# A decoder trunk's opening: x read from a transposed copy, first weights in halves on two queues, norm sums by columns

## What is computed

```
x = x + 1/2 * SwiGLU_1(RMSNorm(x))
h = RMSNorm(x)
x = x + mixers(h) @ W_out
x = x + 1/2 * SwiGLU_2(RMSNorm(x))

rmsnorm(x, gain) = x * rsqrt(mean(x * x, axis=-1) + 1e-6) * gain
swiglu(x, w_gate, w_up, w_down) = (silu(x @ w_gate) * (x @ w_up)) @ w_down
```

## Time and profile before

| | us |
|---|---|
| three timed runs | 1137.74, 1138.39, 1138.44 |
| median | 1138.39 |
| the profiled execution | 1138.71 |
| its span on the core | 1136.9 |

### The profile page before, as it was taken

The page is one execution under the profiler, slowest core; times in us unless marked ns, Lnnn a source line. Parts: engine busy times, 40 slices in busy tenths (PEclk is TensorE's granted clock), DMA queues, the critical chain, the costliest instruction groups (busy, mean ns, idle before and its releaser), DMA issues.

```text
span 1136.9 us, 16092 instructions
## 1 busy us (share of the span) xinstructions
PE 1133.1 (100%) x5975; PEld 966.9 (85%) x5975; DVE 770.4 (68%) x1055; ACT 630.6 (55%) x941; POOL 70.3 (6%) x79
## 2 busy tenths in 40 slices
PE   9999999999999999999999999999999999999999
PEld 7888888888888888888888888888887888888887
DVE  5766666868768676655766856678676695766655
ACT  6644445666674564544564544466766745544542
POOL 3020000202000000000020200002110000000000
PEclk9999999999999999999999999999999999999999
DMA  9956654545544666656566555636445445656521
GB/s 324 319 175 198 187 192 140 185 136 198 148 148 152 219 223 187 193 177 219 172 169 228 185 185 186 200 98 220 148 163 172 182 154 183 222 185 202 193 86 37
DMA packets 138828, 207.34 MB, mean 182 GB/s; under 512 B 6898, under 2 KB 99876, under 8 KB 138756
## 3 DMA queue, kind: packets, MB, share of 16 engines
q1 hardware_dynamic: 137364, 205.02, 55.1%
q0 software_dynamic: 752, 0.79, 0.8%
q10 hardware_dynamic: 640, 0.55, 0.2%
HBM read 205.29 MB, written 1.05 MB: 181 GB/s over the span
## 4 chain that ended last, share of the span: by engine, by line
PE 100%; DVE 0%; issue 0%; POOL 0%; DVEq 0%; POOLq 0%
PE bank L560 28%; PE bank L530 17%; PE bank L534 17%; PE bank L533 17%; PE bank L564 15%; PE bank L546 1%; PE bank L859 1%; PE bank L849 1%; PE bank L830 1%; PE bank L668 1%; PE bank L848 1%; PE bank L877 1%; PE bank L569 0%; PE bank L738 0%; PE bank L735 0%; PE bank L732 0%
## 5 line engine op out<-in xcount | busy, mean ns | idle before, releaser
L1300 DVE TENSOR_TENSOR w_low<-raw,w_high 128x1024 fp32r<-128x1024 f32 x388 | 464.2, 1232 | 281.4 <-ACT w_high L1016 280.8
L1016 ACT ACTIVATE w_high<-raw 128x1024 fp32r<-128x1024 f32 x387 | 393.5, 1055 | 317.8 <-PE bank L564 173.5
L560 PE MATMUL bank<-xT,w_high 128*128 128x512 f32 x1388 | 331.6, 390 | 0.1
L560 PEld LDWEIGHTS bank<-xT,w_high 128*128 128x128 f32 x1388 | 257.0, 188 | 51.2 <-DVE xT L1318 0.2
L564 PEld LDWEIGHTS bank<-xT,w_low 128*128 128x128 f32 x1408 | 175.7, 191 | 3.6
L564 PE MATMUL bank<-xT,w_low 128*128 128x256 f32 x1408 | 178.6, 283 | 0.0
L530 PE MATMUL bank<-w_high,xT 128*128 128x512 f32 (+1 forms) x440 | 171.3, 389 | 0.0
L534 PE MATMUL bank<-w_low,xT 128*128 128x512 f32 (+1 forms) x440 | 168.2, 382 | 0.0
L533 PE MATMUL bank<-w_high,xT 128*128 128x512 f32 (+1 forms) x440 | 168.1, 382 | 0.0
L530 PE MATMUL bank<-w_high,oT_high 128*128 128x512 f32 x418 | 162.6, 389 | 0.0
L534 PE MATMUL bank<-w_low,oT_high 128*128 128x512 f32 x418 | 162.2, 388 | 0.0
(11 more groups left out here) (146 smaller groups left out, 771.5 us busy)
## 6 DMA issues: line engine op xcount, KB each, us to landing
raw<-in_w_in SPq DMA_DIRECT2D x92, 512.0 KB, 4.6
raw<-in_ffn_w_down SPq DMA_DIRECT2D x88, 512.0 KB, 4.3
raw<-in_ffn_w_gate SPq DMA_DIRECT2D x86, 512.0 KB, 4.1
raw<-in_ffn_w_up SPq DMA_DIRECT2D x86, 512.0 KB, 5.0
raw<-in_w_out SPq DMA_DIRECT2D x16, 512.0 KB, 4.4
raw<-in_w_branch_c SPq DMA_DIRECT2D x8, 512.0 KB, 4.0
raw<-in_w_branch_a SPq DMA_DIRECT2D x4, 512.0 KB, 4.1
raw<-in_w_branch_b SPq DMA_DIRECT2D x4, 512.0 KB, 6.0
```

What stands on the lines that cost most here:

```text
L560: return nc.tensor.matmul(bank[b0 + n][:, :], w_high[:, slot, column(k, n)], xT[:, k], start=k == 0, stop=full_last and k == KB - 1)
L1016: act.activation(w_high[:, slot], raw[:, in_slot, (p % 2) * 1024:(p % 2) * 1024 + 1024], ACT.Copy).then_inc(sem["high_ready"], 1)
L1300: dve.tensor_tensor(w_low[:, slot], raw[:, FILL_SLOT[p // 2], (p % 2) * 1024:(p % 2) * 1024 + 1024], w_high[:, slot].bitcast(F32), ALU.sub ...
```

## The change

The host passes two more arrays that hold inputs in another layout: `x_turned`, which is x transposed (1024 x 256), and `gains`, all gains as columns (128 x 2 x 26), with the two constants of lambda in the last column. Then:

- SyncE loads x^T into `x_turned` (the memory of `o_nat`, free at that time) in pieces of 1, 1, 2, 2 and 2 blocks, between the first weights. The weights of row blocks 0 and 1 now come as four DMAs of one row block each, gate on ScalarE's queue and up on SyncE's; `gains` stands second on ScalarE's queue. The rest of the first row comes on SyncE's queue.
- TensorE's first work is 11 products of a tile of ones, and then the real products. All transposes of x in the opening and both transposes of gains are gone. Pair 0 is done a row block at a time: block 0 whole, then block 1.
- VectorE writes both the high and the low of row block 0 of the weights; ScalarE writes the high of row block 1.
- The sum of squares is made otherwise: ScalarE squares x^T (two activations of 128x1024, no sum), VectorE adds the eight blocks with one reduction that reads eight values 256 elements apart for each of 256 results, and TensorE sums over the 128 features with two products with a column of ones (`sum_squares`). ScalarE copies the two columns for GpSimd.
- `turn_row` comes behind the narrow products of pair 4, which is 16 products later than before.
- x in natural layout, which the residual needs, is loaded by GpSimd's queue once chunk 4's hidden values are there; GpSimd's other loads (`trig`, `params`) wait for chunk 2's.

The diff, cut to its core:

```diff
+        def first_rows(engine, k0, nk, landed, parts=(0, 1)):
+
+            v = raw[:, FILL_SLOT[k0 // 4]].rearrange("p (k g c) -> p k g c", k=4, g=2)[:, k0 % 4:k0 % 4 + nk]
+            for g in parts:
+                w = (a["ffn1_w_gate"], a["ffn1_w_up"])[g]
+                engine.dma_start(v[:, :, g], w[0:1, k0 * P:(k0 + nk) * P, 0:FC].rearrange("o (k p) c -> p (o k) c", p=P)
                                  ).then_inc(landed, 16)
...
+            def load_x_turned(piece):
+
+                k0, nk = X_BLOCKS[piece]
+                sp.dma_start(x_turned[:, k0 * S:(k0 + nk) * S].rearrange("p (k s) -> p k s", k=nk),
+                             a["x_turned"][k0 * P:(k0 + nk) * P, :].rearrange("(k p) s -> p k s", p=P)).then_inc(x_turned_landed[piece], 16)
+
+            load_x_turned(0)
+            first_rows(sp, 0, 1, half_landed[0], (1,))
+            load_x_turned(1)
+            first_rows(sp, 1, 1, half_landed[1], (1,))
+            load_x_turned(2)
+            first_rows(sp, 2, 2, fill_landed[FILL_SLOT[0]])
+            load_x_turned(3)
+            first_rows(sp, 4, 2, third_landed)
+            load_x_turned(4)
+            first_rows(sp, 6, 2, fill_landed[FILL_SLOT[1]])
...
+                if layer == 0:
+                    for half in range(HALVES):
+                        pool.dma_start(x[:, half], a["x"][0, half * P:half * P + P, :]).then_inc(x_loaded, 16)
...
-                pe.wait_ge(sem["blocks_high"], 1)
+                pe.wait_ge(block0_high, 1)
                 pe.wait_ge(half_high, 1)
                 for n in range(4):
                     high_part(0, n, w_high, True)
+                pe.wait_ge(half_low, 1)
+                for n in range(4):
+                    high_part(0, n)
+                pe.wait_ge(block0_low, 1)
+                for n in range(4):
+                    low_part(0, n)
+                pe.wait_ge(sem["blocks_high"], 1)
                 pe.wait_ge(sem["high_ready"], value("high_ready", 0, 1))
                 for n in range(4):
                     high_part(1, n, w_high)
-                turn(1, 0, 1)
                 pe.wait_ge(sem["blocks_low"], 1)
-                for k in range(2):
-                    for n in range(4):
-                        low_part(k, n)
+                for n in range(4):
...
-                        if p == 1 and n == 2:
-                            turn(2, 1, 0)
                         for k in (2 * p, 2 * p + 1):
                             full(k, n)
-                    if p == 1:
-                        turn(2, 1, 1)
                     pe.wait_ge(sem["low_ready"], value("low_ready", 0, p + 1))
...
-            def cold_row():
+            def sum_squares():
 
                 pe.wait_ge(sem["up_summed"], 1)
-                turn_row(0, 1, 4)
-                pe.wait_ge(rows_loaded, 16 * 3)
-                nc.tensor.transpose(bank[5][:, 0:GAIN_ROWS], gain_rows[0:GAIN_ROWS, :], ident[0:GAIN_ROWS, 0:GAIN_ROWS]).then_inc(gains_turned, 1)
+                pe.wait_ge(block_squares_summed, 1)
+                for half in range(HALVES):
+                    last = nc.tensor.matmul(bank[4][:, half:half + 1], block_sums[:, half * P:half * P + P], ones[:, 0:1].bitcast(F32),
+                                            start=True, stop=True)
+                last.then_inc(squares_summed, 1)
...
-                        cold_row()
+                        sum_squares()
                     gate_up_wide(layer, p + 2, 2, done + 1, i * 12)
                     gate_up_narrow(layer, p, 0, done + 1, i * 12).then_inc(sem["pair_used"], 1)
+                    if opens and not turned:
+                        turn_row(0, 1, 4)
...
-            pe.wait_ge(zero_ready, 1)
-            warm(WARM_FIRST)
+            pe.wait_ge(ones_ready, 1)
+            warm(WARM)
             pe.wait_ge(ident_ready, 1)
-            pe.wait_ge(first_gains_loaded, 16)
-            nc.tensor.transpose(bank[3][:, 0:16], gain_rows[0:16, :], ident[0:16, 0:16]).then_inc(first_gains_turned, 1)
-            warm(WARM_SECOND)
...
             def cold_start():
 
-                blocks_high(0, ST_FFN1, 0, G_FFN1, (0,))
+                def block(kb):
+
+                    return act.activation(xT_high[:, kb, :], x_turned[:, kb * S:kb * S + S], ACT.Copy,
+                                          scale=gains_all[:, 0, G_FFN1 + kb:G_FFN1 + kb + 1])
+
+                act.wait_ge(gains_loaded, 16)
+                act.wait_ge(x_turned_landed[0], 16)
+                block(0).then_inc(block0_high, 1)
+                act.wait_ge(x_turned_landed[1], 16)
+                block(1).then_inc(sem["blocks_high"], 1)
                 high(0, 0)
-                for n, name in ((1, "mix_norm"), (2, "ffn2_norm")):
-                    act.dma_start(gain_rows[16 * n:16 * n + 16, :], a[name].rearrange("l (k p) -> (l k) p", p=P)).then_inc(rows_loaded, 16)
-                blocks_high(0, ST_FFN1, 0, G_FFN1, (1,))
-                high(0, 1)
-                blocks_high(0, ST_FFN1, 1, G_FFN1, (0,))
-                high(0, 2)
-                blocks_high(0, ST_FFN1, 1, G_FFN1, (1,))
-                high(0, 3)
+                for p in range(1, 4):
+                    act.wait_ge(x_turned_landed[p + 1], 16)
+                    block(2 * p)
+                    block(2 * p + 1).then_inc(sem["blocks_high"], 1)
+                    high(0, p)
+                for first in (0, D):
+                    last = act.activation(x_squares[:, first:first + D], x_turned[:, first:first + D], ACT.Square)
+                last.then_inc(block_squares_ready, 1)
                 high(0, 4)
...
                 p = 4
                 high(0, p + 1)
                 copy_rest(0, 1)
                 high(0, p + 2)
+                high(0, p + 3)
+                act.wait_ge(squares_summed, 1)
+                act.activation(norm_sq, bank[4][:, 0:HALVES], ACT.Copy).then_inc(sem["squares_ready"], 1)
                 copy_row(0, 1)
-                high(0, p + 3)
                 silu_gate(0, 1)
                 high(0, p + 4)
-                cold_rest_gains()
                 high(0, p + 5)
...
+            first_rows(act, 0, 1, half_landed[0], (0,))
+            act.dma_start(gains_all[:, :, :], a["gains"]).then_inc(gains_loaded, 16)
+            first_rows(act, 1, 1, half_landed[1], (0,))
+            act.wait_ge(ones_ready, 1)
+            act.activation(sink_exp_of[0][:, 0:1], ones[:, 0:1].bitcast(F32), ACT.Silu)
...
+            def cold_pairs():
+
+                slot, in_slot = PAIR_SLOT[0], FILL_SLOT[0]
+
+                def block_low(kb):
+                    return dve.scalar_tensor_tensor(xT_low[:, kb, :], x_turned[:, kb * S:kb * S + S], gains_all[:, 0, G_FFN1 + kb:G_FFN1 + kb + 1],
+                                                    xT_high[:, kb, :].bitcast(F32), ALU.mult, ALU.subtract)
+
+                def half_of_low(cols):
+                    return dve.tensor_tensor(w_low[:, slot, cols], raw[:, in_slot, cols], w_high[:, slot, cols].bitcast(F32), ALU.subtract)
+
+                dve.wait_ge(half_landed[0], 32)
+                dve.tensor_copy(w_high[:, slot, 0:512], raw[:, in_slot, 0:512]).then_inc(half_high, 1)
+                dve.drain()
+                half_of_low(slice(0, 512)).then_inc(half_low, 1)
+                dve.wait_ge(block0_high, 1)
+                block_low(0).then_inc(block0_low, 1)
+                dve.wait_ge(sem["blocks_high"], 1)
+                block_low(1).then_inc(sem["blocks_low"], 1)
+                dve.wait_ge(sem["high_ready"], value("high_ready", 0, 1))
+                half_of_low(slice(512, 1024)).then_inc(sem["low_ready"], 1)
+                for p in range(1, 4):
+                    dve.wait_ge(sem["blocks_high"], p + 1)
+                    block_low(2 * p)
+                    block_low(2 * p + 1).then_inc(sem["blocks_low"], 1)
+                    low(0, p)
...
                 p = 4
+                dve.wait_ge(block_squares_ready, 1)
+                dve.tensor_reduce(block_sums, x_squares.rearrange("p (k s) -> p s k", k=KB), axis=AXIS_X, op=ALU.add).then_inc(block_squares_summed, 1)
                 low(0, p)
                 low(0, p + 1)
                 sum_gate(0, 1)
                 sum_up(0, 1)
                 low(0, p + 2)
+                low(0, p + 3)
                 dve.wait_ge(sem["row_ready"], 1)
                 dve.drain()
                 dve.tensor_tensor(gate_scaled[:, :, :], gate_scaled[:, :, :], norm_row[:, :].unsqueeze(1).to_broadcast([P, 2, S]), ALU.mult
                                   ).then_inc(sem["gate_scaled"], 1)
-                low(0, p + 3)
```

More of the change, by code:

```diff
@@ L1642, in _ @@
             dve.sem_inc(sem["low_ready"], CREDIT["low_ready"])
[L1643 to L1644 removed]
             for layer in range(DEPTH):
                 if layer == 0:
[L1648 to L1650 removed]
+                    cold_pairs()
                 else:
```

117 lines of the change are left out of this document (46 added, 71 removed).

## The result

| | before | after |
|---|---|---|
| median, us | 1138.39 (13 runs) | 1140.42 (13 runs) |
| range of the runs | 1137.58 to 1138.69 | 1139.57 to 1142.23 |
| ratio, 95% interval | | 1.0021, 1.0014 to 1.0028 |
| profiled execution | 1138.71 | 1141.37 |
| span | 1136.9 | 1139.6 |

The forecast was 1137.7, range 1136.3 to 1140.4. The change makes the kernel slower, and the time lies 0.02 us above the range.

The account below looks back on a forecast made before the run. TensorE was taken to bound the kernel, with VectorE's chain beside it: of 3.0 us from the opening, two waits left 0.7. From 1138.71 that gave 1138.0, and with the median 0.32 lower 1137.7, range 1136.3 to 1140.4.

Parts of the forecast that it names:

- The ground: Opening: only TensorE's waits count; the early start gives 3.0 us, two waits return all but 0.7.
- number 2: VectorE's reduction of 2048 values behind the squares: 2.3 us, ending at 18.5, bounds 1.2 to 6.1.
- first rival: VectorE's strided reduction at half the contiguous rate: 4.6 us, mark at 34.4, 1140.0 us; chance 0.26.
- the mark: Start of the first down product, 32.81 us before, forecast 32.1; the kernel gains what it gains.
- sign of my forecast: Whole kernel: faster by 0.7 us, from 1138.71 to 1138.0 for the profiled execution.
- step 1: Stream and ScalarE: last first-row weights land at 13.0, pair 3 copied by 14.05, two Squares done at 16.15.
- second rival: Opening's stream no faster, later for the new order: pair 3 at 13.7 gives 1138.4, at 14.5 1139.2; chance 0.13.
- TensorE's own path: TensorE's opening: first product at 5.9, 2.2 earlier; through pairs 4 and 5's wide products at 21.7, 3.0 us gained.
- Steps 4 to 7: Sums to hidden values: sums 0.5 to 22.75, row turned 25.65, Silu ends 27.9, hidden low and mark 32.1.
- gap of 1.5: TensorE ahead of the first down product: own path ends at 30.6, waits 1.5 us for hidden values.
- The full gain: Pairs 8 and 9's lows not in the way, or stream 1 us sooner: mark 30.0, gain 2.8, 1135.6; chance 0.09.
- step 5: Pair 6's wide and pair 4's narrow products, row turned at 25.65; GpSimd's norm has 3 us, isn't late.

Follow-up runs that it names:

- e3: Changed kernel without VectorE's reduction, the norm made from block 0's squares only: 1137.92 us, ratio 0.9996 to the kernel before.
- e2: Changed kernel with the same reduction adding eight neighbouring values, not values 1 KB apart (sums of wrong groups): 1138.47 us, single run.
- e7: e6 with the up half of row block 1 of the weights issued on ScalarE's queue, not SyncE's: 1138.27 us, ratio 0.9999 to before.
- e5: Changed kernel with squares and additions done in pieces as x^T lands, TensorE's order unchanged: 1138.11 us, ratio 0.9999 to before.
- e10: e7 with the products for the sums and the turned row in the middle of pairs 5's and 6's wide products: 1137.33 us, ratio 0.9989 to before.
- e6: e5 with the sums ahead of pair 5's wide products and the turned row behind them: 1138.16 us, ratio 1.0000 to before.
- e1: Changed kernel with three additions of contiguous halves in place of the strided reduction: 1138.19 us, ratio 1.0000 to before.
- e9: Changed kernel with the strided reduction run twice: 1145.56 us, ratio 1.0066.
- e8: Kernel before with the strided reduction added on VectorE ahead of pair 4's low, result unused: 1139.18 us, ratio 1.0008.
- e4: Changed kernel with the sums moved behind pair 6's wide products and the turned row behind pair 5's narrow ones: 1139.79 us, ratio 1.0014.

## Why the prediction was wrong

**The ground held.** What TensorE waits for decides, and it waits where I said: at the sums and ahead of the first down product. Chain and order of the steps came out as written, L1387 is on it, and the change's early start is worth little by itself: 0.4 us with a sum that costs nothing (e3).

**The step that failed is number 2, the size of the reduction.** I put 2.3 us, from a row with contiguous values, and measured 3.92. With contiguous values the term would have been right (2.29). The argument "the engine's pace, not the memory's" against the first rival was wrong; that rival's mechanism is what happened, at 1.7 times and not 2 times the contiguous time. The Trainium skill, SBUF — State Buffer, says under Specifications that SBUF's lines have 16 bytes and that each cross to a new line pays a penalty; e2 beside the changed kernel agrees, with 0.80 ns more for each value, though no run has a step between 4 bytes and 1 KB that would show the line's size. By my own steps 1.6 us more is the mark at 33.7, and 1139.3 for the median.

The mark is 3.0 us later than I said: 1.6 by the reduction, 0.5 by the stream and 1.5 by the clock, less 0.6 in the steps between, which were a little shorter than written.

**A term that I didn't have: the clock.** TensorE's wait of 1.50 us is followed in the profile by 3.4 us at half clock, and 6 runs of 13 have a mean clock of 0.999 and take 1.6 us more. This moves the median, as it sits at the border between both groups: without it the median is 1139.90, inside the range and within 0.2% of no change. So the sign of my forecast fell by the reduction, and the range by the clock.

**Luck.** The first rival's 1140.0 is within 0.4 us of the measured time for partly wrong reasons: it had 0.7 us too much for the reduction, and neither the late stream nor the clock.

**The stream, step 1.** Forecast 13.0 for the last piece, measured 13.5. The start of my chain used the issue at 6.44 of the kernel before; the changed one has an issue more ahead of it (6.95). In the first 6 us it moved 3 x (105 + 231) = 1008 KB against 3 x (73 + 304) = 1131, which is 0.33 us of a full stream of 368 GB/s. I took the small pieces for the cause, since an issue of 128 KB takes 0.43 us on the queue, but that isn't shown: e7, which moved one such issue to the other queue, had only 3 x (91 + 223) = 942 KB. The second rival was this, at a smaller price (13.5 and not 13.7 or 14.5).

**TensorE's own path.** First product 5.09, forecast 5.9. The eleven warm products took 4.26 us in this run, and 5.06 in e5 and e10, where the first product starts at 5.85. Their last three step by 0.23 us each here (4.39 to 5.09), the pace of the 2.4 GHz level, and by 0.43 in e6; the granted clock reads 1.00 in both, so this shows in the steps alone. Pair 1 at 10.22 (9.6): its last piece is issued at 3.60 and not at 3.08, as I had it, and lands 5.4 later. Pair 4 at 18.65 (18.0). All of it lies ahead of a wait.

**Steps 4 to 7.** Sums 0.6 (0.5). Up addition ends at 23.91 (22.2), row turned at 28.88 (25.65), of that 1.7 from steps 1 and 2 and 1.5 from the clock. Mark 35.13 (32.1). The gap of 1.5 that I expected ahead of the mark is 1.17. It doesn't grow with the reduction: it is the length of the step from the turned row to the hidden values, less TensorE's work, and the same 1.17 to 1.18 in e1, e2, e3, e5 and e9.

**The full gain** (third rival) didn't come near. Even e3, without a reduction, and e10, without the wait ahead of the mark, gain 0.4 and 1.2 us.

**What the span has besides the mark.** I took it that the kernel gains what the mark gains. Span less mark is 1104.1 us in the kernel before, e6, e7, e8 and e10, where TensorE doesn't wait at the mark, and 1104.4 to 1104.5 in the changed kernel, e1, e2, e3, e5 and e9, where it waits 1.17 or 1.18 (e4 isn't counted, since its clock fell behind the mark). So the kernels with a wait there lose some 0.4 us more. Most of it lies in the 48 wide products behind the mark: from the mark to the next narrow product that stretch is 10.88 us in the kernel before, e6 and e10, and 11.20 to 11.24 in the changed kernel, e1 and e3, at a granted clock of 1.00. Why they take longer isn't shown. It is a part of why e1, with a mark 1.1 earlier than before, is only 0.1 faster by the medians; the rest is within the spread of single profiled runs.

## What to carry to other kernels

Layout belongs to the price of a reduction: fold contiguous halves, or as each piece lands, rather than walk across rows, and where the trace has no row of the same stride, don't take the contiguous row for the likely price (here it was 1.7 times that). When an opening is made earlier, list who produces each value that the next stage waits for; a stage bounded by such a chain gives next to nothing back for an engine that starts sooner. In this opening the only gain clear of noise came when, on top of that, two short steps of TensorE were moved into the middle of long ones (e10); that placing wasn't tried in the kernel before. A late wait of 1.5 us or more on TensorE should be priced with a share of a clock drop behind it.

## What the runs showed of the hardware

**TensorE's clock fell in more of the runs where its late wait was longer.** Of the kernels with no late wait above 1.2 us only one had a run with a drop; with 1.5 to 2.1 us 10 of 24 runs had one, and with 5.1 us all 5. Longest wait of TensorE in the profiled run, and runs with a mean clock below 1.000: 0.81 us (e8), none of 11, and 0.81 at 10.8 us (e10), none of 11; 1.18 (e1), 1 of 11; 1.18 (e3), none of 11; 1.51 (e5) and 1.47 (e6), both at 10.6 us, none of 11 each; 1.18 at 8.2 us (e7), none of 11; 1.50 at 24 us (changed kernel), 6 of 13; 2.13 (e4), 4 of 11; 5.10 (e9), 5 of 5. In the profiled runs a drop took 3.4 us (changed kernel, e4) or 6.8 (e9). Between the medians of the runs with and without it are 1.6 us in the changed kernel and 1.2 in e4. The length of the wait isn't all: 1.47 to 1.51 us at 10.6 us has none in 22 runs, where 1.50 at 24 us has 6 in 13. What decides, between these places or within one kernel, isn't shown.

**A small step of GpSimd waits for the end of VectorE's low of weights.** The same L473 on two values takes 0.19 us or up to 1.18. In the slow cases it begins in the middle of VectorE's low of weights and ends 0.05 us behind it. In the changed kernel the pair of lows on VectorE:

```profile
23.84 2.34 DVE L1306 TENSOR_TENSOR w_low<-raw,w_high 128x1024 fp32r<-128x1024 f32 x2
```

ends at 26.18, and the step on GpSimd at 26.23:

```profile
25.05 1.18 POOL L473 TENSOR_SCALAR small<-small 128x2 f32<-128x2 f32 x1 [19.94 <-ACT small L1096]
```

In e10 it is 23.90 and 23.95, in e9 29.81 and 29.86; in e3 the lows are through at 23.15, and L473 from 23.06 takes 0.19. Beside the reduction, which reads one tile where the low reads two, the step isn't held. In e8 the reduction runs from 18.21 to 22.11, and inside it:

```profile
20.28 0.19 POOL L464 TENSOR_SCALAR small<-small 128x2 f32<-128x2 f32 x1 [16.83 <-ACT scratch L1043]
```

The Trainium skill, SBUF — State Buffer, section Terms, says that VectorE and GpSimd lock a shared pair of ports for a full instruction and that the loser fully blocks. The rows beside the lows agree, and the price of a step on two values was up to 1.0 us more. In the changed kernel TensorE didn't wait for it, so step 5 of the prediction stands; in e6 it did.
